# Projection pieces of a hybrid trunk kernel issued unit by unit from the attention on through the retention, with the first rotation and the last transposes at other places

## The reference

```python
proj = x @ w_in[l] + b_in[l]
(fq, fk, fv, ff, rq, rk, rv, rg, hf, hi, hq, hg, mq, gate) = jnp.split(proj, SPLIT_POINTS, axis=-1)
o_fox = forgetting_attention(_heads(fq), _heads(fk), _heads(fv), ff)
o_ret = retention(_heads(rq), _heads(rk), _heads(rv), _heads(rg))
o_hg = hgrn2(_heads(hq), _heads(hi), _heads(hf), _heads(hg), lb_all[l], hgrn_norm_g[l])
mk, mv = jnp.split(mem @ w_mem_kv[l], 2, axis=-1)
o_mem = memory_attention(_heads(mq), _heads(mk), _heads(mv))
up = jnp.einsum('bsnc,ncd->bsnd', branches, w_branch[l])
gates = jax.nn.sigmoid(gate.reshape(B, S, N_BRANCH, D))
mixed = jnp.sum(gates * up, axis=2) @ w_out[l]
x = _layer_norm(DEEPNORM_ALPHA * x + mixed, ln_g[l, 0], ln_b[l, 0])
x = _layer_norm(DEEPNORM_ALPHA * x + grouped_moe(x, w_router, b_router, w_e_in[l], w_e_out[l]), ln_g[l, 1], ln_b[l, 1])
```

## Time and profile before

| what | before |
|---|---|
| median of 3 runs | 3137.23 us (3121.53 to 3142.09) |
| the profiled execution, time | 3123.07 us |
| the profiled execution, span in the profile | 3121.4 us |
| TensorE busy | 2824.7 us, 90% of the span |
| VectorE busy | 1544.4 us, 49% |
| ScalarE busy | 1163.0 us, 37% |
| mean granted clock of TensorE | 0.948 of full |
| attention and retention of layer 0 | about 165 to 480 us of the span |
| attention and retention of layer 1 | about 1711 to 2026 us of the span |

### The profile page before, as it was taken

How to read it: one execution, slowest core, us unless ns; L and a number is a source line. 1 busy time by engine, 2 the same in 40 slices (tenths; PEclk the granted TensorE clock), 3 DMA queues, 4 the chain that set the end, 5 groups by cost and what they waited for, 6 DMA issues and landing times.

```text
span 3121.4 us, 47244 instructions
## 1 busy us (share of the span) xinstructions
PE 2824.7 (90%) x15748; PEld 1486.9 (48%) x15749; DVE 1544.4 (49%) x2477; ACT 1163.0 (37%) x1845; POOL 260.1 (8%) x240
## 2 busy tenths in 40 slices
PE   5999799999999699999579997999999995999994
PEld 3555454554444444445345554545544453444452
DVE  3243464343345567656533335533443455577665
ACT  3234403222232156556432444042222321466663
POOL 0000000000000011222310000000000000122223
PEclk8999899999999799999779998999999996999996
DMA  6200101111114379977622010111111153699974
GB/s 251 68 1 1 55 1 51 51 35 52 51 61 176 128 281 344 316 238 245 217 100 68 1 37 19 31 38 35 51 37 53 62 195 139 231 337 336 317 255 141
DMA packets 150902, 398.56 MB, mean 128 GB/s; under 512 B 13700, under 2 KB 58928, under 8 KB 149904
## 3 DMA queue, kind: packets, MB, share of 16 engines
q1 hardware_dynamic: 133104, 327.59, 28.9%
q0 software_dynamic: 14816, 54.12, 7.2%
q10 hardware_dynamic: 2816, 14.68, 1.3%
HBM read 343.91 MB, written 56.63 MB: 128 GB/s over the span
## 4 chain that ended last, share of the span: by engine, by line
PE 74%; issue 7%; DVE 5%; DMA 4%; PEld 3%; ACT 2%; DVEq 2%; SPq 1%; POOLq 0%; POOL 0%; PEldq 0%; ACTq 0%
PE PA L2001 13%; PE PA L1580 10%; PE PA L1582 10%; PE PA L1581 10%; PE PB L2020 6%; PE PC L1561 3%; PE PB L1581 3%; PE PB L1582 3%; PE PB L1580 3%; DMA RA<-x_rows,BR 2%; PE PD L1580 1%; PE PD L1582 1%; PE PD L1581 1%; PEld PA L1580 1%; PEld PA L1582 1%
## 5 line engine op out<-in xcount | busy, mean ns | idle before, releaser
L2001 PE MATMUL PA<-XT,RA 128*128 128x512 f16 x2304 | 510.0, 382 | 10.4 <-DVE RA L1001 6.2
L1580 PE MATMUL PA<-XT,W 128*128 128x512 f16 x1216 | 463.3, 381 | 6.2 <-DVE W L1001 5.5
L1581 PE MATMUL PA<-XT,W 128*128 128x512 f16 x1216 | 463.0, 381 | 0.0
L1582 PE MATMUL PA<-XT,W 128*128 128x512 f16 x1216 | 462.8, 381 | 0.0
L2001 PEld LDWEIGHTS PA<-XT,RA 128*128 128x128 f16 x2304 | 225.6, 98 | 277.5 <-issue 13.5
L1001 DVE SCALAR_TENSOR_TENSOR XT<-OT,XT 128x1024 f16<-128x1024 f32 x256 | 294.7, 1220 | 44.8 <-ACT XT L879 44.8
L1001 DVE SCALAR_TENSOR_TENSOR W<-W 128x512 f16<-128x512 f32 (+2 forms) x320 | 199.4, 661 | 178.3 <-ACT W L648 166.8
L805 ACT ACTIVATE WK<-PA,bT 128x512 f32<-128x512 f32 x128 | 88.0, 687 | 494.8 <-PE PA L1582 494.2
L2020 PE MATMUL PB<-W,WK 128*128 128x512 f16 x1152 | 260.1, 383 | 6.6 <-DVE W L1001 4.4
L879 ACT ACTIVATE XT<-OT 128x1024 f16<-128x1024 f32 x240 | 230.6, 1042 | 41.9 <-issue 41.8
L1235 DVE SCALAR_TENSOR_TENSOR MKV<-WK,PB 128x512 f32<-128x512 f32 x96 | 66.0, 688 | 339.5 <-PE PB L1582 339.5
(11 more groups left out here) (348 smaller groups left out, 4223.7 us busy)
## 6 DMA issues: line engine op xcount, KB each, us to landing
OT<-in_w_e_in_dram SPq DMA_DIRECT2D x256, 512.0 KB, 7.4
RA<-in_w_e_out_dram SPq DMA_DIRECT2D x128, 512.0 KB, 8.9
W<-in_w_in_dram SPq DMA_DIRECT2D x104, 512.0 KB, 4.7
W<-in_w_branch_dram SPq DMA_DIRECT2D x32, 256.0 KB, 4.9
W<-in_w_out_dram SPq DMA_DIRECT2D x16, 512.0 KB, 5.2
x_rows<-RC SPq DMA_DIRECT2D x16, 512.0 KB, 5.0
y_sum<-RC SPq DMA_DIRECT2D x16, 512.0 KB, 5.8
OT<-y_sum SPq DMA_DIRECT2D x16, 512.0 KB, 3.8
```

Source lines behind the costliest of these rows:

```text
L1580: mm(dst, lhs(0), rhs(0), start=first, stop=False)
L1581: mm(dst, lhs(0), rhs(1), start=False, stop=False)
L1582: return mm(dst, lhs(1), rhs(0), start=False, stop=last)
L2001: q = mm(PA[:, half, :], ROWS[:, a, k * P:(k + 1) * P], EIS[:, b, k, half * HALF:(half + 1) * HALF], start=k == 0 and a + b == 0, stop=k = ...
```

## The change

- `half_of` numbers the halves unit by unit: first all tiles of unit 4, then of unit 5, then of 6 and of 7. Before, units 4 and 5 took turns.
- Every attention tile takes 16 pieces, tile 7 too, and 2 more (`FILL_0`) stand behind its last transposes. The retention takes its pieces from the same `fill`, 7 at each of two places a tile (5 at the second place of tile 0), so that halves no longer end where a place ends. The pieces stay 240 a layer behind the two halves made ahead of the attention.
- Unit 6 is split in attention tiles 4 to 6 (3, 3 and 2 steps), unit 7 in retention tiles 0 to 2 (3, 3 and 2), unit 8 in retention tiles 5 to 7 (2, 2 and 1). VectorE evicts in the retention whatever halves are done by each of two places (`halves_at`).
- The first rotation stands in attention tile 7, between the memory attention's maximum and the inversion of its sums. Its buffers, and those of the normalization, move from `WK` to `OT`.
- The last `times_v_mem` stands behind the first transposes of the retention. ScalarE's silu stands behind its first copy in the retention, and VectorE waits for it only before the product that reads it.
- The transpose of the last retention output stands behind gate group 0, on ScalarE and VectorE behind the first tanh and the first product. Gate group 0 waits, before it writes PB, for the last tile's statistics (`r_var`).

```diff
-        def filled(t):
-
-            return (3, 2, 3, 3, 2, 3) if t < NT - 1 else (0, 0, 0, 3, 2, 3)
+        FILL_ATT = (3, 2, 3, 3, 2, 3)
+        FILL_0 = 2
 
         def half_of(x):
 
-            return (4 + x % 2, 1 + x // 2, 26 + x) if x < 2 * (NT - 1) else (6, 0, 40)
+            if x < 2 * (NT - 1):
+                return 4 + x // (NT - 1), 1 + x % (NT - 1), 26 + x
+            x -= 2 * (NT - 1)
+            return 6 + x // NT, x % NT, 40 + x
+
+        def halves_at(t, place):
+
+            return (2 * KD * NT + FILL_0 * ((t, place) == (0, 1)) + 7 * (2 * t + place)) // KD
+
+        def fill_ret(t, place):
+            return 7 - (FILL_0 if (t, place) == (0, 1) else 0)
```

On ScalarE, in the attention, at the start of the retention and behind it:

```diff
                     if t >= 1:
                         att_high(t - 1, 0)
-                    if last_tile:
-                        high_parts(6, range(2, 4))
+                    if 4 <= t < NT - 1:
+                        high_parts(6, range(3 * (t - 4), min(8, 3 * (t - 3))))
                     softmax_exp(t, 1)
...
                 for t in range(NT):
                     act.wait_ge(r_tr, at(r_tr, t + 1))
                     nc.scalar.copy(WK[:, 1792:2304], PC[:, 0, :]).then_inc(r_qk, 1)
+                    if t == 0:
+                        att_high(NT - 1, 3)
+                        act.wait_ge(pj_v, at(pj_v, 24))
+                        nc.scalar.activation(RN[:, :, 3 * BW:4 * BW], RN[:, :, 3 * BW:4 * BW], ACT.Silu).then_inc(r_sil, 1)
+                        act.preload_act_table_set("natural_log_exp_and_others")
                     if t >= 1:
                         copy_ot(2 * NT + t - 1, 1, t - 1)
+                    if t <= 2:
+                        high_parts(7, range(3 * t, min(8, 3 * t + 3)))
+                    if t >= NT - 3:
+                        high_parts(GATE_U, range(2 * (t - NT + 3), min(5, 2 * (t - NT + 4))))
                     act.wait_ge(r_var, at(r_var, t + 1))
...
-                high_parts(GATE_U)
-                copy_ot(3 * NT - 1, 1, NT - 1)
...
                 gate_tanh(0)
+                copy_ot(3 * NT - 1, 1, NT - 1)
                 decays(0)
```

On VectorE:

```diff
                     softmax_max(t, 1)
+                    if 4 <= t < NT - 1:
+                        low_parts(6, range(3 * (t - 4), min(8, 3 * (t - 3))))
...
                     softmax_max_mem(t)
+                    if t == NT - 1:
+                        rotate(0)
                     sums_inverse(2 * t + 1)
...
+                    while done < halves_at(t, 2):
+                        evict_half(done)
+                        done += 1
+                    if t <= 2:
+                        low_parts(7, range(3 * t, min(8, 3 * t + 3)))
+                    if t >= NT - 3:
+                        low_parts(GATE_U, range(2 * (t - NT + 3), min(5, 2 * (t - NT + 4))))
                     v.wait_ge(r_o, at(r_o, t + 1))
```

On TensorE:

```diff
-                times_v_mem(NT - 1)
                 pe.wait_ge(rs_cp, at(rs_cp, 2 * NT))
+                fill(FILL_0)
...
                 for t in range(NT):
                     pe.wait_ge(r_rot, at(r_rot, t + 1))
+                    if t == 0:
+                        pe.wait_ge(pt_cp, at(pt_cp, NT * ATT + 1))
...
-                    if t >= 1:
-                        project_pair(6, t, 0, 40 + 2 * t)
+                    if t == 0:
+                        times_v_mem(NT - 1)
+                    fill(fill_ret(t, 0))
...
-                    project_pair(6, t, 1, 41 + 2 * t)
+                    fill(fill_ret(t, 1))
...
-                pe.wait_ge(r_on, at(r_on, NT))
-                transpose_o(3 * NT - 1, ON[:, (NT - 1) % 2, :])
...
                 gate_group(0)
+                pe.wait_ge(r_on, at(r_on, NT))
+                transpose_o(3 * NT - 1, ON[:, (NT - 1) % 2, :])
                 running_sums(0)
```

More of the change, by code:

```diff
@@ L733, in _ @@
                 for t in range(NT):
-                    last_tile = t == NT - 1
                     if t >= 1:
                         copy_pt(t - 1, H)
-                    if last_tile:
-                        high_parts(6, range(0, 2))
                     softmax_exp(t, 0)
@@ L759, in _ @@
                     copy_weights(2 * t)
-                    if last_tile:
-                        high_parts(7, range(0, 4))
                     copy_row(2 * t + 1)
@@ L1179, in rotate, with group_norm_stats @@
                     tt(heads(KDC[t % 2]), heads(ROT[:, BW:2 * BW]), over(co("kdec"), HD), ALU.mult).then_inc(r_rot, 1)
-                rotate(0)
                 for t in range(NT):
                     if t >= 1:
-                        evict_proj(40 + 2 * t, HN[:, t, 0:HALF], C_HF)
+                        normalize(2 * t - 2)
+                    softmax_max(t, 0)
+                    if t >= 1:
+                        att_low(t - 1, 0)
+                    softmax_max(t, 1)
+                    if 4 <= t < NT - 1:
+                        low_parts(6, range(3 * (t - 4), min(8, 3 * (t - 3))))
+                    if t >= 1:
+                        normalize(2 * t - 1)
+                        att_low(t - 1, 3)
+                    softmax_max(t, 2)
+                    softmax_max(t, 3)
+                    evict_half(2 * t)
+                    sums_inverse(2 * t)
+                    softmax_max_mem(t)
+                    if t == NT - 1:
+                        rotate(0)
+                    sums_inverse(2 * t + 1)
+                    evict_half(2 * t + 1)
+                normalize(2 * NT - 2)
+                att_low(NT - 1, 0)
+                normalize(2 * NT - 1)
+                att_low(NT - 1, 3)
+                QKT, QDT, STM = WK[:, 1792:2304], WK[:, 2304:2560], WK[:, 2560:3072]
+                def group_norm_stats(o, done):
+                    nc.vector.tensor_reduce(st[:, 0:4].rearrange("p (j a) -> p j a", j=2), o, AX.X, ALU.add)
+                    v.drain()
+                    ts(st[:, 0:4], st[:, 0:4], 1.0 / HD, None, ALU.mult)
+                    v.drain()
+                    tt(paired(CEN), o, over4(st[:, 0:4]), ALU.subtract)
+                    v.drain()
+                    tt(SQ, CEN, CEN, ALU.mult)
+                    v.drain()
+                    nc.vector.tensor_reduce(st[:, 4:8], heads(SQ), AX.X, ALU.add)
+                    v.drain()
+                    ts(st[:, 4:8], st[:, 4:8], 1.0 / HD, GN_EPS, ALU.mult, ALU.add).then_inc(done, 1)
+                done = 2 * NT
+                for t in range(NT):
+                    while done < halves_at(t, 1):
+                        evict_half(done)
+                        done += 1
                     v.wait_ge(r_qk, at(r_qk, t + 1))
@@ L1748, in transpose_o @@
                     q.then_inc(ot_tr, 1)
-                chunks = iter(range(KD * (2 * NT - 1)))
+                chunks = iter(range(KD * (4 * NT - 2)))
                 def fill(n):
@@ L1764, in fill @@
                             q.then_inc(pj, 1)
-                            if u < 6 and t == NT - 1:
+                            if t == NT - 1:
                                 pe.drain().then_inc(w_used, 1)
                 for t in range(NT):
-                    f = filled(t)
+                    f = FILL_ATT
                     scores(t, 0)
@@ L1851, in gate_group @@
                     pe.wait_ge(g_mul, at(g_mul, g + 1))
+                    if g == 0:
+                        pe.wait_ge(r_var, at(r_var, NT))
                     for j in range(2):
```

91 lines of the change are left out of this document (18 added, 73 removed).

## The result

| | before | after |
|---|---|---|
| median | 3131.43 us (4 runs, 3121.53 to 3142.09) | 3090.2 us (4 runs, 3088.0 to 3094.66) |
| profiled execution, time and span | 3123.07, 3121.4 us | 3088.0, 3086.3 us |
| mean granted clock | 0.948 | 0.952 |

The ratio is 0.9873, 95% interval 0.9845 to 0.99. Four more executions of the changed kernel gave 0.9891 (0.9876 to 0.9906). The change is worth 1.1 to 1.3%, 35 to 41 us; the forecast was 1.2%, 38 us. Both intervals lie clear of 1.

A forecast was written before the change was run, and what follows sets the result against it. TensorE bounds the kernel (busy 2824.7 of 3121.4 us), so only its idle time and clock can give. Terms of 19.0 us per layer, 38 us for both, off the median of 3137.23 gave 3099 us; range 3072 to 3120.

The forecast's parts named there:

- the term of tiles 4 and 5: Attention tiles 4 and 5: third high part of unit 6 delays the second exponential 1.35 us a tile; loss 2.7 us per layer.
- One of the prediction's own signs of being wrong: Signs: retention tile above 13 us, last wait of 10 us, or half clock behind the waits in tiles 4 and 5.
- Tile 7 and the seam: Attention tile 7 to first retention scores: waits shrink or go, gains 3.2, 3.1 and 11.1 us; clock 2.9 us, per layer.
- the 0 for the clock: Attention tiles 4 and 5: half clock behind the two lengthened waits taken to cost 0.
- the kept 3.0: Attention tiles 4 and 5: possible half-clock cost of 1.5 us for each of two waits, kept for the range.
- The retention: Retention tiles: with 14 pieces a tile takes 12.4 us without a pause; cost 0.
- The slack of 0.4 us: Retention tile: last output ready at 4.56 us, TensorE comes for its transpose after 5.0 us.
- The rival of the retention: Retention: VectorE becomes the bound, up to 9.1 us per layer lost; gain 20 us, 3117 us; chance 0.10.
- The end: End of retention: ScalarE's chain starts 3.9 us sooner, gain 3.9; new wait 6.5 us ahead of running_sums; clock loss 2.5.
- The first, that the clock takes a part back: Waits in tiles 4, 5, 7 and the new wait bring half clock, 5.5 us per layer; gain 27 us, 3110; chance 0.17.
- Late evictions: Retention: halves finding their bank full stop TensorE, 28 us per layer lost against 19 won; 3155 us; chance 0.02.

The follow-up runs named there:

- e2b_rotation_back: Changed kernel with the first rotation behind the attention again and the silu ahead of the retention's first copy; 3114.99 us.
- e3_no_extra_two: Changed kernel without the 2 extra pieces behind the last attention transposes (FILL_0 = 0), which stand in retention tile 0 instead; 3087.27 us.
- e1_parts_spread: Changed kernel with the third weight step of attention tiles 4 and 5 moved behind the fourth softmax; 3085.82 us, ratio 0.9852.
- e7_split_5_9: Changed kernel with the 14 pieces of a retention tile split 5 and 9 instead of 7 and 7; 3108.21 us.
- e8_more_ahead: On top of both repairs, two pieces in attention tiles 3 to 7 moved ahead of the second head's transposes; 3072.0 us, ratio 0.9807.
- e4_transposes_first: Changed kernel with the last retention output's transposes ahead of gate group 0 again on TensorE; 3085.89 us.
- both repairs: Changed kernel with the edits of e1_parts_spread and e5_group_cover together; 3063.78 us, ratio 0.9795, and again 3065.94 us, 0.9796.
- e5_group_cover: Changed kernel with gate group 1 ahead of the first running sums and group 2 ahead of TensorE's next wait; 3081.65 us, ratio 0.9845.

## Why the prediction was right

Its 38 us are 34.4 in the stretch and 35 to 41 between the medians. The 3.6 us missing in the stretch are the term of tiles 4 and 5, 4.7 us too small over both layers; the other differences, each of at most 1.1 us, add up to 1.1 us the other way. The medians are less exact than that: the forecast of 3099 us started from a median of 3137.23 before, which is 3131.43 with a fourth run. One of the prediction's own signs of being wrong did come: half clock followed the waits in tiles 4 and 5, in the second of them in every layer. So the gain was right while the part on the clock there was not; the error is small beside 38 us, and other terms made up a part of it by luck.

- **Tile 7 and the seam.** Predicted 3.2 + 3.1 + 11.1 + 2.9 = 20.3 us; measured, without the pieces, 17.9 + 2.5 = 20.4 and 18.2 + 2.7 = 20.9. The wait left in tile 7 is 2.46 us, said 2.5. `e2b_rotation_back` shows the places of the rotation and the silu to carry 8.8 us of it, and `e3_no_extra_two` that the two extra pieces are cover and carry 1.3.
- **Unit 6 in tiles 4 and 5.** This is the term that was mis-sized: 2.7 us taken, 6.5 and 3.6 measured. Its mechanism was right, as the trace shows the third high part waiting and `e1_parts_spread` takes the loss away. The waits grew by 1.16 us each, said 1.35. Wrong was the 0 for the clock, taken although the one case at hand, the 2.06 us of tile 6 in layer 0, had half clock behind it: in place of it stand 1.6 us in one layer and 4.5 in the other, so the kept 3.0 was also 1.5 too little for the worse layer.
- **The retention.** A tile takes 12.43 us, said 12.4, without a pause, but for tile 3 (below). The slack of 0.4 us was 0.15 to 0.57. The rival of the retention needs that slack gone; `e7_split_5_9` took it away, and it cost 7.2 us a layer, by the chain and not by VectorE's load.
- **The end.** Predicted a gain of 3.9 us, a new wait of 6.5 and 2.5 us lost to the clock; measured 4.5 and 4.3 us, 6.45 us (three loads of 1.28 us and three passes of 1.91, as priced) and 2.1 us. By the figure of the Trainium skill, ScalarE: Activation LUTs, What ACT_TABLE_LOAD costs, of about 2.66 us per switch with a drain, the estimate of the wait was about 10.5 us; the trace disagrees, as the next activation follows a load of 1.28 us within 0.02 us (in ScalarE's timeline of the changed kernel):

```profile
467.68 1.28 ACT L792 ACT_TABLE_LOAD   x1
468.98 1.91 ACT L792 ACTIVATE RC<-RC 128x2048 f32<-128x2048 f32 x1
```

- **What had no term.** Tiles 0 to 3 became 0.4 us longer and retention tiles 1 to 6 0.5 us. Both changes lie in the tile in which a unit now ends in the middle (retention tile 3 takes 12.95 us). Behind the last piece of a unit the program drains TensorE (`pe.drain()` in `fill`), and the trace has a pause there that no other engine ends:

```profile
405.12 0.38 PE L1582 MATMUL PA<-W,XT 128*128 128x512 f16 x1
405.85 0.38 PE L1580 MATMUL PA<-W,XT 128*128 128x512 f16 x1 [0.35 <-issue]
```

  From start to start this is 0.73 us where it is 0.22 without the drain, the 0.5 us in question. Unit 4's pause, also 0.35 us, stood in attention tile 6 before and stands in tile 3 now; tile 6 became 0.3 us shorter. The pauses lie where the drains stand, but no run left a drain out.
- **The rivals.** The first, that the clock takes a part back, is half true: half clock followed in tiles 4, 5 and 7 and behind the new wait. In tile 7 eight transposes took 1.73 us behind the 2.46 us; behind the 3.76 us of before they took 1.94, so there it was no new loss. Late evictions did not occur; `e8_more_ahead` shows the mechanism at another place, at 0.8 to 1.4 us a half.

The step that I had argued loosely is the moved transposes at the end. I counted the 4.5 us as going and the chain's wait as coming; `e4_transposes_first` shows that this order alone bought nothing and cost 2.0 us a layer.

## What to carry to other kernels

On an engine that executes in order, price a moved instruction by what is queued behind it and when its own input comes: two weight steps were free in a gap of 1.9 us, and the third, which waits for another engine's answer, was not. Cover a stop with work that is already there, and when it is moved ahead, move with it whatever empties its buffer. A stop of TensorE costs its length, and behind most of the stops of 2.06 us and more in these traces half clock took another 1.4 to 2.9 us. So a stop of several microseconds is worth breaking up, and one that can't be removed is better placed so that another wait absorbs what runs slowly behind it.

## What the runs showed of the hardware

The clock was the surprise. I had taken a wait of 2.5 us for harmless or worth 1.5 us at most. The counts of half clock (0.50 granted), over the layers of all thirteen profiled executions in which the wait in question is there:

| wait of TensorE | half clock behind it |
|---|---|
| 1.11 and 1.59 us (tiles 4 and 5 of the kernel before, of `e1_parts_spread` and of both repairs) | in none of 8 layers |
| 2.06 us (tile 6) | in 7 of 22, 1.6 us lost |
| 2.27 us (tile 4 of the changed kernel) | in 4 of 14, 1.5 to 1.6 us lost |
| 2.46 us (tile 7 of the changed kernel and of the repairs) | in 20 of 20; no layer without it to compare |
| 2.75 us (tile 5 of the changed kernel) | in 14 of 14, 1.6 us or 2.8 to 2.9 us lost |
| 3.11 us (ahead of L1733 in tile 7 of the kernel before) | in none of 2 layers |
| 4.55 us (L1747 ahead of the group, kernel before and `e4_transposes_first`) | in 4 of 4; in `e4_transposes_first` absorbed by the wait for ScalarE's chain |
| 6.16 us (rotation back) | in both layers, 2.5 us lost |
| 6.45 us (ahead of `running_sums`) | in all 12 layers, 1.4 to 2.8 us lost |
| 9.20 us (ahead of L1802 in the kernel before) | in both layers |

The tile's length tells it: 50.9 to 51.3 us for tiles 4 and 5 without half clock, 54.8 to 54.9 or 57.5 to 57.8 with it, and 28.6 to 28.9 or 30.2 to 30.5 for tile 6, never between. In all four layers with 57.5 us or more, tile 6 had half clock too. Which of the two a given layer gets differs from one execution to the next of the same kernel, so the wait's length alone does not decide it. The wait of 3.11 us says so too: behind it, in a stretch of the kernel before, the clock is full (columns as in the earlier trace rows).

```profile
356.30:361.20 4.90, 3.76 (x49) 3.06 (x49) 0.93 (x2) 1.66 (x4) 0.00 (x0) 1.00 0.02 5
```

What else decides it, these runs don't show. Half clock can also reach into the stretch from ahead of it: in layer 1 of `e5_group_cover` and of `e2b_rotation_back`, attention tile 0 took 19.36 and 19.70 us instead of 17.34.

The Trainium skill, TensorE: Matmul & The Clock Gate, Why this matters for your kernels, warns of idle gaps between bursts. These traces agree that half clock follows such gaps, and differ in the length: it came behind 2.06 to 2.75 us, shorter than the gaps that the page names, and did not come behind one of 3.11 us.
